# Sample attention of the odd layer: cached keys and values loaded during the projection, values as weights

## What is computed

```python
def odd_sample(x, buf_k, buf_v, w_in, sinks, w_out):
    pos = PAST_LEN + jnp.arange(Q)
    q, k, v = swa_qkv(x, w_in, pos)                     # 16 query heads, 4 key/value heads of 64
    kc = jnp.concatenate([buf_k, k], axis=1)            # 128 cached + 8 new
    vc = jnp.concatenate([buf_v, v], axis=1)
    ...
    o = sink_attend(q.reshape(...), kc[:, None], vc[:, None], mask, sinks)
    return o.reshape(Bd, Q, ODD_MIX) @ w_out, (kc[:, -WINDOW:], vc[:, -WINDOW:])

def sink_attend(q, k, v, mask, sinks):
    s = jnp.einsum('bnqkgd,bnckd->bnkgqc', q, k) * HEAD_DIM ** -0.5
    s = jnp.where(mask, s, -jnp.inf)
    m = jnp.maximum(s.max(-1), sink)
    p = jnp.exp(s - m)
    p = p / (p.sum(-1) + jnp.exp(sink - m))
    return jnp.einsum('bnkgqc,bnckd->bnqkgd', p, v)
```

## Time and profile before

| | |
|---|---|
| median of 3 runs | 3263.23 us (3261.16 to 3281.02) |
| the profiled execution's own time | 3274.18 us |
| its span | 3272.5 us |
| TensorE busy | 2939.8 us, 90% |
| VectorE busy | 1775.2 us, 54% |
| ScalarE busy | 1204.3 us, 37% |
| DMA, mean over the span | 82 GB/s |

### The profile page before, as it was taken

One profiled execution on the slowest core, in us unless ns is written; L12 is line 12 of the kernel. 1 busy time (PEld: TensorE's weight loads), 2 busy tenths in 40 slices (PEclk: granted clock), 3 DMA queues, 4 the chain that ended last, 5 costly groups with the idle time before them and its releaser, 6 DMA issues. The chain is left out here.

```text
span 3272.5 us, 50986 instructions
## 1 busy us (share of the span) xinstructions
PE 2939.8 (90%) x18874; PEld 2460.4 (75%) x18893; DVE 1775.2 (54%) x3186; ACT 1204.3 (37%) x2655; POOL 1040.3 (32%) x1097
## 2 busy tenths in 40 slices
PE   7999999678999869999989969869996999998995
PEld 7889777354566569999977759836664999997784
DVE  2168443484898463333359873324546333334988
ACT  2222543433555443333333441114444333333342
POOL 2200222440111024444346534400001444443555
PEclk8999887788999989999999979959998999999998
DMA  4211102443110022222173432230001222226343
GB/s 124 74 41 42 27 27 76 135 125 101 48 39 27 20 65 80 80 80 80 54 244 105 162 103 40 66 112 23 27 27 53 79 80 80 80 67 207 120 160 119
DMA packets 269998, 269.61 MB, mean 82 GB/s; under 512 B 61779, under 2 KB 197158, under 8 KB 269734
## 3 DMA queue, kind: packets, MB, share of 16 engines
q1 hardware_dynamic: 263254, 255.57, 25.1%
q0 software_dynamic: 6512, 10.89, 1.1%
HBM read 212.24 MB, written 55.89 MB: 82 GB/s over the span
## 5 line engine op out<-in xcount | busy, mean ns | idle before, releaser
L2228 PE MATMUL ffn0u_ps<-ffn0u_x_hi,ffn0u_whi 128*128 128x272 f32 x1232 | 358.8, 291 | 20.4 <-DVE ffn0u_wlo L2331 10.6
L2228 PE MATMUL ffn1u_ps<-ffn1u_x_hi,ffn1u_whi 128*128 128x272 f32 x1232 | 358.4, 291 | 20.0 <-DVE ffn1u_wlo L2331 10.9
L2228 PE MATMUL ffn0u_ps<-ffn0u_x_hi,ffn0u_wlo 128*128 128x272 f32 x1232 | 356.4, 289 | 0.0
L2228 PE MATMUL ffn1u_ps<-ffn1u_x_hi,ffn1u_wlo 128*128 128x272 f32 x1232 | 356.2, 289 | 0.0
L221 PE MATMUL ine_ps<-ine_w_hi,ine_x_hi 128*128 128x256 f32 (+2 forms) x864 | 262.0, 303 | 5.2 <-DVE ine_w_lo L237 5.0
L2228 PEld LDWEIGHTS ffn0u_ps<-ffn0u_x_hi,ffn0u_whi 128*128 128x128 f32 x1232 | 234.6, 190 | 22.5 <-DVE ffn0u_wlo L2331 21.2
L2228 PEld LDWEIGHTS ffn1u_ps<-ffn1u_x_hi,ffn1u_whi 128*128 128x128 f32 x1232 | 234.2, 190 | 22.2 <-DVE ffn1u_wlo L2331 20.9
L221 PE MATMUL ine_ps<-ine_w_hi,ine_x_lo 128*128 128x256 f32 (+2 forms) x864 | 249.4, 289 | 0.0
L221 PE MATMUL ine_ps<-ine_w_lo,ine_x_hi 128*128 128x256 f32 (+2 forms) x864 | 248.9, 288 | 0.0
L2228 PEld LDWEIGHTS ffn0u_ps<-ffn0u_x_hi,ffn0u_wlo 128*128 128x128 f32 x1232 | 234.4, 190 | 0.0
L2228 PEld LDWEIGHTS ffn1u_ps<-ffn1u_x_hi,ffn1u_wlo 128*128 128x128 f32 x1232 | 234.4, 190 | 0.0
(11 more groups left out here) (559 smaller groups left out, 7902.5 us busy)
## 6 DMA issues: line engine op xcount, KB each, us to landing
ffn0u_raw<-in_ffn_w_gu_dram SPq DMA_DIRECT2D x44, 512.0 KB, 5.1
ffn0d_w<-in_ffn_w_down_dram SPq DMA_DIRECT2D x88, 256.0 KB, 2.9
ffn1u_raw<-in_ffn_w_gu_dram SPq DMA_DIRECT2D x44, 512.0 KB, 5.4
ffn1d_w<-in_ffn_w_down_dram SPq DMA_DIRECT2D x88, 256.0 KB, 3.0
scratch_a<-ffn0u_u SPq DMA_DIRECT2D x44, 272.0 KB, 2.1
scratch_a<-ffn1u_u SPq DMA_DIRECT2D x44, 272.0 KB, 2.1
aT<-scratch_a SPq DMA_DIRECT2D x8, 1024.0 KB, 10.8
aT<-scratch_a SPq DMA_DIRECT2D x10, 768.0 KB, 9.2
```

The lines of the kernel that those rows point to most:

```text
L2228: last = nc.tensor.matmul(ps[:, bank + h, 0:TOK2], wp, xp, start=(begins and k == 0 and n == 0), stop=(k == KH - 1 and n == 2), skip_group ...
```

## The change

- The loads of `Kb`, `Vb`, `band_f` and `sink` are issued by SP in `odd_in_projection`, behind the weight pieces of chunk 2, into buffers that now live through both stages; SP waits for them at the end of that stage.
- VectorE multiplies the probabilities by the reciprocal of the sums before TensorE transposes them (semaphore `p_scaled`).
- In the values matmuls `Vb` (128x128) and `Vn` (8x128) are the weights and 64 columns of probabilities move, so a result has head dimensions as rows and (g, q) as columns.
- Eight small copies on ScalarE (batches 0 to 3) and eight on VectorE (batches 4 to 7) place the useful halves in `YT_sample`. The scaling of the heads, the stores, the load, the transposes and their copy go.

```diff
@@ odd_in_projection, SP
                     if c == 0:
                         sp.dma_start(cs[:, :, :], C["cos"]).then_inc(cin, 16)
                         sp.dma_start(sn[:, :, :], C["sin"]).then_inc(cin, 16)
+                    if c == 2:
+                        Kb, Vb, band_f, sink = window
+                        sp.dma_start(Kb[:, :, :], A["state_swa_k"][0].rearrange("b w k d -> w b (k d)")).then_inc(window_in, 16)
+                        sp.dma_start(Vb[:, :, :], A["state_swa_v"][0].rearrange("b w k d -> w b (k d)")).then_inc(window_in, 16)
+                        sp.dma_start(band_f[:, :], C["bands"]).then_inc(window_in, 16)
+                        sp.dma_start(sink[:, :], bass.AP(A["swa_sinks"].tensor, 0, [[1, 16], [0, DEC_SEQ], [1, 1]]),
+                                     allow_slow_non_contiguous=True).then_inc(window_in, 16)
+                sp.wait_ge(window_in, 64)
@@ swa_sample, SP
-                sp.dma_start(Kb[:, :, :], A["state_swa_k"][0].rearrange("b w k d -> w b (k d)")).then_inc(buf_in, 16)
-                sp.dma_start(Vb[:, :, :], A["state_swa_v"][0].rearrange("b w k d -> w b (k d)")).then_inc(buf_in, 16)
-                sp.dma_start(band_f[:, :], C["bands"]).then_inc(cin, 16)
-                sp.dma_start(sink[:, :], bass.AP(A["swa_sinks"].tensor, 0, [[1, 16], [0, DEC_SEQ], [1, 1]]),
-                             allow_slow_non_contiguous=True).then_inc(cin, 16)
...
-                sp.wait_ge(y_done, 1)
-                for b in range(NB):
-                    sp.dma_start(bass.AP(scr.tensor, b * DEC_SEQ * D, [[HD, 16], [D, DEC_SEQ], [1, HD]]), yq[:, b, :]).then_inc(y_out, 16)
-                sp.wait_ge(y_out, 16 * NB)
-                sp.dma_start(Y[:, :], scr).then_inc(y_in, 16)
                 sp.wait_ge(stored, 32 + 32 * NB)
@@ TensorE
-                pe.wait_ge(buf_in, 32)
...
-                pe.wait_ge(e_done, 1)
+                pe.wait_ge(p_scaled, 1)
...
-                        r = slice(64 * m, 64 * m + 64)
-                        o = ps[r, b // 4, (b % 4) * P:(b % 4 + 1) * P]
-                        nc.tensor.matmul(o, PT[:, b, r], Vb[:, b, m * P:(m + 1) * P], start=True, stop=False)
-                        last = nc.tensor.matmul(o, PTn[:, b, r], Vn[:, b, m * P:(m + 1) * P], start=False, stop=True)
-                last.then_inc(o_done, 1)
-                pe.wait_ge(y_in, 16)
-                for k in range(KD):
-                    last = nc.tensor.transpose(ps[:, 5, k * NS:(k + 1) * NS], Y[:, k * P:(k + 1) * P], I64)
-                last.then_inc(yt_done, 1)
+                        r, c = slice(64 * m, 64 * m + 64), (b % 4) * P + 64 * m
+                        o = ps[:, b // 4, c:c + 64]
+                        nc.tensor.matmul(o, Vb[:, b, m * P:(m + 1) * P], PT[:, b, r], start=True, stop=False)
+                        last = nc.tensor.matmul(o, Vn[:, b, m * P:(m + 1) * P], PTn[:, b, r], start=False, stop=True)
+                    if b % 4 == 3:
+                        last.then_inc(o_done, 1)
+
+            def place_heads(op, half, done):
+                for v in range(2):
+                    for odd in range(2):
+                        for m in range(2):
+                            src = ps[64 * v:64 * v + 64, half, :].rearrange("d (b m w g o q) -> d m w o g b q", b=4, m=2, w=2, g=2, o=2)
+                            dst = XT[64 * odd:64 * odd + 64, 4 * m + 2 * v:4 * m + 2 * v + 2, 32 * half:32 * half + 32]
+                            op(dst.rearrange("d g (b q) -> d g b q", b=4), src[:, m, v, odd, :, :, :]).then_inc(done, 1)
@@ ScalarE
-                act.wait_ge(yt_done, 1)
-                nc.scalar.copy(XT[:, :, :], ps[:, 5, :].rearrange("p (k t) -> p k t", k=KD)).then_inc(yt_copied, 1)
-                act.wait_ge(yt_copied, 1)
+                act.wait_ge(o_done, 1)
+                place_heads(nc.scalar.copy, 0, y_act)
+                act.wait_ge(y_act, 8)
@@ VectorE
-                dve.wait_ge(cin, 32)
                 nc.vector.tensor_copy(band[:, :], band_f[:, :]).then_inc(ready, 1)
...
-                dve.wait_ge(pt_done, 1)
-                nc.vector.tensor_copy(PT[:, :, :], ps[:, 3:5, :].rearrange("p c (b t) -> p (c b) t", b=4)).then_inc(pt_copied, 1)
                 dve.wait_ge(e_done, 1)
                 link(nc.vector.tensor_tensor(rs[:, :], sm[:, :], es[:, :], ALU.add))
                 link(nc.vector.reciprocal(rs[:, :], rs[:, :]))
-                dve.wait_ge(o_done, 1)
-                for kv in range(4):
-                    r, v = slice(32 * kv, 32 * kv + 32), kv % 2
-                    ins = nc.vector.tensor_tensor(
-                        yq[r, :, :], ps[r, 0:2, :].rearrange("p c (b d) -> p (c b) d", b=4)[:, :, v * HD:(v + 1) * HD],
-                        rs[r, :].unsqueeze(2).to_broadcast([32, NB, HD]), ALU.mult)
-                ins.then_inc(y_done, 1)
+                nc.vector.tensor_tensor(Pb[:, :, :], Pb[:, :, :], rs[:, :].unsqueeze(2).to_broadcast([P, NB, NK]),
+                                        ALU.mult).then_inc(p_scaled, 1)
+                dve.wait_ge(pt_done, 1)
+                nc.vector.tensor_copy(PT[:, :, :], ps[:, 3:5, :].rearrange("p c (b t) -> p (c b) t", b=4)).then_inc(pt_copied, 1)
+                dve.wait_ge(o_done, 2)
+                place_heads(nc.vector.tensor_copy, 1, y_dve)
+                dve.wait_ge(y_dve, 8)
```

More of the change, by code:

```diff
@@ L2874, with odd_in_projection @@
 SCOLS = 1536
-def odd_in_projection(nc, st, C, w, XT, H):
+def odd_in_projection(nc, st, A, C, w, XT, H, window):
     tag = "ino"
@@ L2895, in odd_in_projection @@
         bank_done, act_evac, dve_evac = sem("bank_done"), sem("act_evac"), sem("dve_evac")
+        window_in = sem("window_in")
         cin, rot_c, rot_s, rot_done = sem("const_in"), sem("cos_done"), sem("sin_done"), sem("rotated")
@@ L3440, in _, with swa_sample @@
                 dve.wait_ge(t_dve, counts[1])
-def swa_sample(nc, st, A, C, O, H, XT):
+def swa_sample(nc, st, A, O, H, XT, window):
     NB, NK = DEC_BATCH, P + DEC_SEQ
-    scr = nc.dram_tensor("scratch_ys", (NS, D), F32, kind="Internal").ap()
+    Kb, Vb, band_f, sink = window
     T = H[:, NT, :]
@@ L3451, in swa_sample @@
         sem = lambda n: st.sem(f"sws_{n}")
-        Kb, Vb, Vn = sb("Kb", [P, NB, 256]), sb("Vb", [P, NB, 256]), sb("Vn", [DEC_SEQ, NB, 256])
+        Vn = sb("Vn", [DEC_SEQ, NB, 256])
         KT, kn = sb("KT", [P, NB, 2, NK]), sb("kn", [P, 2, NS])
         qz = sb("qz", [P, NB, 2, 2, 4, DEC_SEQ])
-        band_f, band, identb = sb("bandf", [P, NK]), sb("band", [P, NK], BF16), sb("identb", [P, P], BF16)
-        sink = sb("sink", [P, 1])
+        band, identb = sb("band", [P, NK], BF16), sb("identb", [P, P], BF16)
         mx, nm, es, sm, rs = (sb(n, [P, NB]) for n in ("mx", "nm", "es", "sm", "rs"))
@@ L3459, in swa_sample @@
         PTn = sb("PTn", [DEC_SEQ, NB, P])
-        yq, Y = sb("yq", [P, NB, HD]), sb("Y", [NS, D])
         ps = ctx.enter_context(nc.psum_tensor("sws_ps", [P, 8, 512], F32))
-        buf_in, cin, vn_in, ready, dch = sem("buffers_in"), sem("const_in"), sem("v_new_in"), sem("ready"), sem("dve_step")
+        vn_in, ready, dch = sem("v_new_in"), sem("ready"), sem("dve_step")
         q_done, q_copied, k_done, k_copied = sem("qT"), sem("qT_copied"), sem("kT"), sem("kT_copied")
         s_done, m_done, e_done, pt_done, pt_copied = sem("scores"), sem("max"), sem("probs"), sem("pT"), sem("pT_copied")
-        o_done, y_done, y_out, y_in, yt_done, yt_copied, stored = (sem("o"), sem("y"), sem("y_out"), sem("y_in"), sem("yT"),
-                                                                   sem("yT_copied"), sem("stored"))
+        p_scaled, o_done, y_act, y_dve, stored = sem("p_scaled"), sem("o"), sem("y_act"), sem("y_dve"), sem("stored")
         def score(b, n=NK):
@@ L3627, in rest @@
         H = mix.enter_context(nc.sbuf_tensor("H1", [P, TILES, SCOLS], F32))
-        odd_in_projection(nc, st, C, A["w_in_odd"][0], XT, H)
+        window = [mix.enter_context(nc.sbuf_tensor(f"window_{n}", sh, F32)) for n, sh in (
+            ("Kb", [P, DEC_BATCH, 256]), ("Vb", [P, DEC_BATCH, 256]), ("bandf", [P, P + DEC_SEQ]), ("sink", [P, 1]))]
+        odd_in_projection(nc, st, A, C, A["w_in_odd"][0], XT, H, window)
         place.close()
@@ L3631, in rest @@
         YTs = mix.enter_context(nc.sbuf_tensor("YT_sample", [P, KD, NS], F32))
-        swa_sample(nc, st, A, C, O, H, YTs)
+        swa_sample(nc, st, A, O, H, YTs, window)
         st.end_phase()
```

## The result

| | before | after |
|---|---|---|
| median of 20 runs each, taken in turns | 3271.99 us (3255.66 to 3281.02) | 3250.27 us (3242.27 to 3264.71) |
| span of the profiled execution | 3272.5 us | 3246.8 us |

The ratio is 0.9937, interval 0.9923 to 0.9951: 20.6 us less (16 to 25), where 25.6 were forecast. The time itself, 3250, lies above the range. The profiled spans differ by 25.7 us, the number of the forecast, but not for its reasons.

A forecast was written before the change was run, and what follows sets the result against it. TensorE was taken to bound the kernel, so only its waits in the odd layer's sample attention pay. The terms -8.9, +1.75, -5.7 and -12.75 sum to -25.6 us, from 3263.2 to 3237 rounded down, range 3226 to 3246.

The forecast's parts named there:

- What bounds the kernel; no overlap across the barriers: TensorE bounds the kernel; barriers isolate the odd layer's sample attention, so what its chain loses, the kernel loses.
- Term 1: Key, value, band and sink loads moved to the projection: -8.9 us in the stage; cost there 0, at worst +1.
- Term 2: Scaling of the probabilities on VectorE, now ahead of TensorE's transposes: +1.75 us (bounds 1.6 and 1.9).
- Term 3: Values as weights in the values matmuls: 64 records at 0.20 us, 12.8 us for 18.5, -5.7 us.
- Term 4: Heads' way by DRAM after the values goes, 14.25 us, replaced by eight VectorE copies: -12.75 us.
- The sum: The four terms of the sample stage together: -25.6 us, time 3237; bounds 3236 to 3242; chance 0.80 with C.
- The base: Starting time of the whole kernel: 3263.2 us, the median of the runs shown, from which the saving was taken.
- A: Rival: clock stays at 1.00 into the scores and returns for the values; another 9 us, time 3228; chance 0.11.
- B: Rival: weight loads set the values' pace, 0.32 us a record; Term 3 is +2.0, time 3245; chance 0.07.
- C: Rival: loads disturb the projection or heads' copies cost more; +1 to +3 us, 3239 to 3241; within the sum's 0.80.
- D: Rival: the next stage does not get its clock back; up to 3301 us with 90 us of such work; chance 0.02.
- Within 1%: Whole kernel's time changes by no more than 1% either way; chance 0.84.

The follow-up runs named there:

- e4: The kernel before with only the loads of cached keys, values, band and sinks moved to the odd projection; ratio to the kernel before 0.998.
- e3: The kernel before with only its values matmuls sorted by weight rows within each half; 3256.7 us in one profiled run, stage 55.28 us.
- e1: The changed kernel with the same 32 values matmuls sorted by weight rows within each half; ratio to the kernel before 0.9919, stage 41.90 us.
- e5: e3 with the two halves of the result's rows written one after the other instead of in turns; 3254.7 us in one profiled run.
- e2: The changed kernel, order kept, with new values and their probabilities padded by zero rows to 128; 3253.2 us in one profiled run.
- e7: e1 plus filler matmuls with unread results in TensorE's idle time, 12 of them at the next stage's start; ratio to the kernel before 0.9913.
- e8: e6 plus filler matmuls with unread results, 12 of them at the next stage's start; ratio to the kernel before 0.9884.
- e9: e8 without the 12 filler matmuls at the next stage's start; 3227.23 us, ratio to the kernel before 0.9871.
- e10: e9 with the next stage's band and sinks loaded in the sample stage; 3229.75 us, ratio to the kernel before 0.9873.
- e6: The kernel before with loads moved, values matmuls sorted, heads scaled in halves by VectorE and transposed on TensorE without DRAM; ratio 0.989.

## Why the prediction was right and where it failed

- **What bounds the kernel; no overlap across the barriers.** Right: what the stage lost, 20.06 us, the kernel lost (20.6, interval 16 to 25).
- **Term 1**, -8.9: measured -8.87. The projection paid nothing: chunk 2's first split waited 8.25 us for 7.79, within the cover of 3.9. The move done alone (e4) gave back 2.0 us later in the stage, 1.3 of them in values that ran at 0.50; in the whole change nothing of the kind shows.
- **Term 2**, +1.75: measured +1.75, the product at 1.29.
- **Term 3**, -5.7: measured -0.26. This is the step that failed, by its size. The forecast took 0.118 us a record from line 3180 (the row shown works out to 0.107) for a form that has the same shapes there, but all weights with 128 rows. In this stage every second matmul has 8. The trace of before held the warning in the same paragraph: 0.181 for a form that, in one run of equal rows, takes 0.064 (e3). I read it as the price of 128 moved columns and halved it in the lower bound; two thirds of it were the changes of rows. With these gone, e1 measures 12.8 us, the very value of term 3, at 0.121 and 0.225 in place of 0.118 and 0.20.
- **Term 4**, -12.75: measured -12.70.
- **The sum.** Without term 3's -5.7 the terms make -19.9; the stage shows -20.06; the rest is small (the values -0.26, the copies and key transposes -0.23, the transposes of the probabilities +0.19). The forecast's -25.6 agrees with the two profiled spans only by luck: 5.4 us that were gained ahead of the stage, nearly all in unchanged code, fill the gap.
- **The base.** The miss in the time is 3250.3 - 3237 = 13.3 us. Of it 8.8 are the base: three runs had the median 3263.2, twenty have 3272.0. 3.9 are the saving, 25.6 against 21.7 between the medians, and 0.6 the rounding down. The range took 20 us of spread between three runs as the spread of a run, and left little of it for the median that it started from.
- **Rivals.** A (clock 1.00): no; the scores ran at 0.50 again. B: its time, 3245, is nearer than mine, but its cause is mostly not the one: with loads of 128 columns a record takes 0.121 us at 1.00 and 0.225 at 0.50 in e1, not 0.32, and e5 leaves them a part of 0.026 at 1.00 together with what moves. C and D: no; the tail took 1.55 us, and the next stage's first 14.4 us run at 0.51 as before. "Within 1%" held.

## What to carry to other kernels

Price a matmul from rows that have the same neighbours, not only the same shape, and where a kernel alternates weights of different row counts, sort them first: that one reordering took 12 us from a stage of 67, more than half of what the whole change brought. Here the waits that were read from a timeline, with what queues behind them, came out to a tenth of a us; the saving that is left to forecast lies in paces that change with order and clock. Where unchanged code varies by 10 us between executions, forecast the difference, and give the base a spread of its own.

## What the runs showed of the hardware

Where f32 matmuls with 128-row and 8-row weights alternate, a record took 0.181 us at 1.00 and 0.308 at 0.50 in both forms (before, after). Sorted, it took 0.121 and 0.225 with weights of 128 columns (e1), 0.064 and 0.119 with weights of 64 (e3). So the alternation cost 0.060 us a record at 1.00 in the one form and 0.117 in the other, not one fixed amount; zero rows up to 128 removed it (0.215 at 0.50, e2). Matmuls with 64-column weights that take turns between the two halves ran at 0.064 us a record where one half after the other took 0.095 (both at 1.00). In e7 the granted clock fell from 1.00 to 0.50 within a stretch in which TensorE was busy 3.10 of 3.10 us, and in after it stayed at 0.50 over 7.08 busy of 7.10 us. Matmuls whose result nobody reads, 18 of them, went with a stage of 28.0 us in place of 36.6, in three profiles of three (e8, e9, e10 against e6).
